# A decoder step with stick-breaking attention: keys moved to partitions, later keys summed by triangular products, and the order of products in every weight multiplication

## What is computed

```
z          = q . k / sqrt(64)
log_keep   = log_sigmoid(-z)                      # = -(max(z,0) + ln(1 + exp(-|z|)))
after[s]   = sum of log_keep over the keys between s and t
weight[s]  = exp(log_sigmoid(z) + after)          # = exp(z + log_keep[s] + after[s])
out        = sum over s of weight[s] * v[s]
```

## Time and profile before

| | us |
|---|---|
| median of 3 runs | 2714.1 (2711.0 to 2717.55) |
| the profiled execution, its own time | 2701.8 |
| its span, first to last instruction | 2700.0 |
| attention of layer 1 and head norm (from the last matmul of the gemm before to the first of the output gemm) | 1888.8 to 2146.6 |
| of that, stick-breaking units | about 1964 to 2128 |
| mean granted TensorE clock, share of full | 0.962 |

### The profile page before, as it was taken

One profiled execution on the slowest core, in us unless ns is written; L12 is line 12 of the kernel. 1 busy time (PEld: TensorE's weight loads), 2 busy tenths in 40 slices (PEclk: granted clock), 3 DMA queues, 4 the chain that ended last, 5 costly groups with the idle time before them and its releaser, 6 DMA issues. The chain is left out here.

```text
span 2700.0 us, 44621 instructions
## 1 busy us (share of the span) xinstructions
PE 2566.6 (95%) x18322; PEld 2437.0 (90%) x18322; DVE 884.3 (33%) x1549; ACT 773.1 (29%) x963; POOL 807.9 (30%) x204
## 2 busy tenths in 40 slices
PE   7999999997789999999999999999788799999997
PEld 7999999985589999999999999999455599999997
DVE  3221223686742211223322022211655432202234
ACT  4222223223123222224322122311444432212232
POOL 3333333320023333433333333333000033333332
PEclk9999999997789999999999999999887799999998
DMA  4222223411112222222222222333321022222122
GB/s 150 90 77 91 78 69 115 76 63 37 44 65 87 78 82 90 78 68 79 103 78 78 102 78 69 108 118 125 107 85 48 15 88 78 69 98 82 61 87 74
DMA packets 66901, 220.57 MB, mean 82 GB/s; under 512 B 14006, under 2 KB 31286, under 8 KB 51194
## 3 DMA queue, kind: packets, MB, share of 16 engines
q1 hardware_dynamic: 55968, 202.35, 21.7%
q10 hardware_dynamic: 10842, 16.96, 2.2%
HBM read 207.95 MB, written 11.33 MB: 81 GB/s over the span
## 5 line engine op out<-in xcount | busy, mean ns | idle before, releaser
L439 POOL TENSOR_TENSOR wl<-raw,wr 128x2048 fp32r<-128x2048 f32 (+2 forms) x200 | 807.7, 4038 | 1866.8 <-ACT wr L868 1866.8
L449 PE MATMUL ps<-xr,wr 128*128 128x256 f32 (+1 forms) x2432 | 726.2, 299 | 27.5 <-POOL wl L439 20.2
L451 PE MATMUL ps<-xr,wl 128*128 128x256 f32 (+1 forms) x2432 | 723.3, 297 | 0.0
L450 PE MATMUL ps<-xl,wr 128*128 128x256 f32 (+1 forms) x2432 | 723.1, 297 | 0.0
L449 PEld LDWEIGHTS ps<-xr,wr 128*128 128x128 f32 x2432 | 464.5, 191 | 31.3 <-issue 24.2
L449 PE MATMUL ps<-x2r,wr 128*128 128x256 f32 (+1 forms) x1664 | 491.3, 295 | 0.8 <-POOL wl L439 0.8
L451 PE MATMUL ps<-x2r,wl 128*128 128x256 f32 (+1 forms) x1664 | 489.7, 294 | 0.0
L450 PE MATMUL ps<-x2l,wr 128*128 128x256 f32 (+1 forms) x1664 | 489.4, 294 | 0.0
L450 PEld LDWEIGHTS ps<-xl,wr 128*128 128x128 f32 x2432 | 464.4, 191 | 0.2
L451 PEld LDWEIGHTS ps<-xr,wl 128*128 128x128 f32 x2432 | 463.9, 191 | 0.0
L868 ACT ACTIVATE wr<-raw 128x2048 fp32r<-128x2048 f32 (+1 forms) x200 | 351.5, 1758 | 372.5 <-PE ps L451 299.1
(11 more groups left out here) (310 smaller groups left out, 1857.9 us busy)
## 6 DMA issues: line engine op xcount, KB each, us to landing
raw<-in_up SPq DMA_DIRECT2D x88, 1024.0 KB, 4.8
raw<-in_down SPq DMA_DIRECT2D x32, 768.0 KB, 4.1
raw<-in_mixin SPq DMA_DIRECT2D x24, 1024.0 KB, 4.8
raw<-in_down SPq DMA_DIRECT2D x32, 640.0 KB, 3.8
raw<-in_ple SPq DMA_DIRECT2D x16, 640.0 KB, 3.9
raw<-in_mixout SPq DMA_DIRECT2D x8, 1024.0 KB, 5.0
kc<-in_kc SPq DMA_DIRECT2D x32, 256.0 KB, 3.7
vc<-in_vc SPq DMA_DIRECT2D x32, 256.0 KB, 4.0
```

Source lines behind the costliest of these rows:

```text
L439: e.tensor_tensor(wl[s][:, 0:p.width], raw[s][:, 0:p.width], wr[s][:, 0:p.width].bitcast(F32), ALU.subtract).then_inc(S(f"w_split{s}"), 1)
L449: e.matmul(out, wrt, xrt, start=first, stop=False)
L450: e.matmul(out, wrt, xlt, start=False, stop=False)
L451: return e.matmul(out, wlt, xrt, start=False, stop=last)
```

## The change

Stick-breaking attention is recast with the 128 keys on partitions and queries in columns, both heads of a pair in one unit: 20 units in place of 36. For a block of keys `i` the queries from that block on are its columns (512 - 128 i). The running sum along keys becomes products on PE: a triangular matrix `after` within the block and a matrix of minus ones `later` for each later block, accumulated in PSUM; DVE adds the sums to the logits, ACT takes exp, and the weights are already in the layout for the product with the values, which now gives feature-major output. Transposes, their copies and the scan go away. The mask is added by DVE when it copies the scores out of PSUM. For the sample group the cached keys and values are the stationary operand (128 x 128) and 16 or 32 query columns stream. The head norm of the differential half is cut in six parts of 384 columns and worked inside the ticks of stick-breaking, and so are the rounding and rest of its four tiles; the output gemm reads `okr`, `oql`, which lie over `ok` and `oq`, in place of `xr`, `xl`.

In every gemm the six matmuls of a step are issued in another order: for wr·xr, then wr·xl, then wl·xr, the first bank and the second bank each. The constants are loaded in two parts; the second is loaded by SP ahead of the bias strips in layer 1. Cache jobs 6 and 7 wait for stick-breaking's own units.

```diff
-                            for hf in range(2):
-                                x0, x1 = (0, CUT) if hf == 0 else (CUT, T)
-                                mm = mm3(piece(u, hf), wr[s][:, a:b], wl[s][:, a:b],
-                                         r[:, x0:x1], q[:, x0:x1], k == 0, k == kn_ - 1)
+                            for n_, (w_, x_) in enumerate(((wr[s], r), (wr[s], q), (wl[s], r))):
+                                for hf, (x0, x1) in enumerate(((0, CUT), (CUT, T))):
+                                    mm = e.matmul(piece(u, hf), w_[:, a:b], x_[:, x0:x1],
+                                                  start=k == 0 and n_ == 0, stop=k == kn_ - 1 and n_ == 2)
...
+    UNITS = [(hh, i) for hh in range(HEADS) for i in (3, SAMPLES, 2, 1, 0)]
+    OC_AT, OC_COLS = (6, 7, 11, 12, 16, 17), 3 * P
...
-                e.wait_ge(S("values_done"), SAMPLE_AT[job - 2] + 1)
+                if job < PAIRS + 2:
+                    e.wait_ge(S("values_done"), SAMPLE_AT[job - 2] + 1)
+                else:
+                    e.wait_ge(S("stick_values"), STICK_AT[job - 2 - PAIRS] + 1)
...
+        def stick_scores(v):
...
+            if i < SAMPLES:
+                for c in range(2):
+                    r = slice(64 * c, 64 * c + 64)
+                    mm = e.matmul(ps[:, s + c, 0:w], ok[1][r, hh, i * P:(i + 1) * P], oq[1][r, hh, i * P:SEQ],
+                                  start=True, stop=True)
+            else:
...
+                for g in range(NPG):
+                    for h_ in range(HEADS):
+                        for b in range(2):
+                            o, q = g * P + h_ * 32 + b * 16, h_ * P + (2 * hh + b) * 16
+                            e.matmul(ps[:, s, o:o + 16], kc[job % 2][:, b, h_, g, :], qst[:, q:q + 16],
+                                     start=True, stop=True)
...
+        def stick_sums(v):
...
+            if i < SAMPLES:
+                for j in range(i, TM):
+                    o, at = (j - i) * P, STICK_COLS[j]
+                    for c in range(2):
+                        mm = e.matmul(ps[:, s + c, o:w], C("after" if j == i else "later"),
+                                      stick[hh % 2][:, c, at:at + w - o], start=j == i, stop=j == TM - 1)
+            else:
+                for g in range(NPG + 1):
+                    for q in range(g, NPG + 1):
+                        mm = e.matmul(ps[:, s, g * P:(g + 1) * P], C("after" if q == g else "later"),
+                                      stick_s[:, q * P:(q + 1) * P], start=q == g, stop=q == NPG)
...
+        def stick_values(v):
...
+                for o0, o1 in ((0, P), (P, w))[:TM - i]:
+                    for c in range(2):
+                        f = (2 * hh + c) * 64
+                        mm = e.matmul(ps[64 * c:64 * c + 64, 6, i * P + o0:i * P + o1], ov[1][:, i, f:f + 64],
+                                      wt[:, c, o0:o1], start=i == TM - 1, stop=i == 0 and o0 > 0)
```

The order of the calls in a tick, with k = tick - 20, on PE:

```diff
+        for tick in range(TICKS.stop):
...
+                stick_scores(k)
...
+                stick_sums(k - 2)
...
+                stick_values(k - 3)
+            if k in OC_AT:
...
+                e.matmul(oc_ps, ones[:], sq[:, 0:OC_COLS], start=True, stop=True).then_inc(S("oc_ss"), 1)
```

On ACT, where `stick_soft(k, 0)` is |z|, `stick_soft(k, 1)` is exp and ln, and `stick_weights(k - 2)`, the exp, waits for `stick_add(k - 2)` of DVE:

```diff
+        for tick in range(TICKS.stop):
...
+                stick_soft(k, 0)
...
+                stick_weights(k - 2)
...
+                stick_soft(k, 1)
...
+        for j in range(HEADS, KD):
+            mix_round(j)
```

On DVE, where `stick_logs` makes -log_keep once the ln is there and `stick_add` adds the sums of PE to the logits:

```diff
+        for tick in range(TICKS.stop):
...
+                stick_mask(k)
...
+                stick_out(k - 4)
...
+                stick_logs(k - 1)
...
+                stick_add(k - 2)
```

More of the change, by code:

```diff
@@ L51, with offsets @@
 BLK = 2048
[L54 to L62, removed]
+CONST = dict(ident=128, cm=128, blk_ml=64, blk_col=8, sel=4 * 128)
+CONST2 = dict(neg_incl=128, dneg=4 * 64, fold=64, half0=1, half1=1, stick_neg=128, own_neg=4 * 32,
+              after=128, later=128)
+def offsets(widths):
+    at, o = {}, 0
+    for n, w in widths.items():
+        at[n] = o
+        o += w
+    return at, o
+COFF, CW = offsets(CONST)
+COFF2, CW2 = offsets(CONST2)
 PARAM = dict(gains=9 * KD, conv_w=TM * TAPS, conv_b=TM, ln_g=TM, ln_b=TM, gate_b=2, head_g=TM,
@@ L219, in build @@
     ov = [sb(f"ov{i}", [P, ST, DA], at=z) for i in range(2)]
+    STRIP_AT = z[0]
     strip = sb("strip", [P, HEADS, SEQ], at=z)
@@ new lines, in build, with width1, of_unit, logits @@
+    N1 = len(UNITS)
+    STICK_AT = [v for v, m in enumerate(UNITS) if m[1] == SAMPLES]
+    TICKS = range(N, N + N1 + 5)
+    OC_AT, OC_COLS = (6, 7, 11, 12, 16, 17), 3 * P
+    def width1(v):
+        i = UNITS[v][1]
+        return 3 * P if i == SAMPLES else SEQ - i * P
+    def of_unit(v, banks):
+        w = width1(v)
+        return banks[:, 0, 0:w] if UNITS[v][1] == SAMPLES else banks[:, :, 0:w]
+    def logits(v):
+        return of_unit(v, stk[v % 4][:])
+    def keep_logs(v):
+        hh, i = UNITS[v]
+        return stick_s[:] if i == SAMPLES else stick[hh % 2][:, :, STICK_COLS[i]:STICK_COLS[i] + width1(v)]
@@ L734, in turn_rows @@
+        def turn_rows(u):
+            src, w, bank = rows[u % 4], width(u), 4 + u % 2
+            e.wait_ge(S("probs_done"), u + 1)
+            if u >= 2:
+                e.wait_ge(S("probsT_copied"), u - 1)
+            for b in range((w + P - 1) // P):
                 wb = min(P, w - b * P)
-                if other is None:
-                    mm = e.transpose(ps[0:wb, 4 + u % 2, b * P:(b + 1) * P], src[:, b * P:b * P + wb], C("ident"))
+                if MAPS[u][1] < SAMPLES:
+                    mm = e.transpose(ps[0:wb, bank, b * P:(b + 1) * P], src[:, b * P:b * P + wb], C("ident"))
@@ L844, in _ @@
+        e.wait_ge(S("stick_weights"), N1)
+        e.wait_ge(S("oc_root"), 2 * len(OC_AT))
+        gemm(("out", 1), lambda tile, k: (okr[k // TM][:, k % TM, :], oql[k // TM][:, k % TM, :]), lambda tile, k: ("mix_ready", KD + k + 1) if tile == 0 else None)
         ffn(3, 6)
@@ new lines, in stick_add, with stick_logs @@
+        def stick_add(v):
+            e.wait_ge(S("stick_sums"), v + 1)
+            e.tensor_tensor(logits(v), logits(v), of_unit(v, ps[:, 4:6, :]), ALU.add).then_inc(S("stick_added"), 1)
+        def stick_logs(v):
+            hh, i = UNITS[v]
+            e.wait_ge(S("stick_soft"), 3 * v + 3)
+            if i == TM - 1 and hh >= 2:
+                e.wait_ge(S("stick_sums"), UNITS.index((hh - 2, 0)) + 1)
+            if i == SAMPLES and hh:
+                e.wait_ge(S("stick_sums"), STICK_AT[hh - 1] + 1)
+            e.scalar_tensor_tensor(keep_logs(v), logits(v), 0.0, of_unit(v, soft1[v % 2][:]), ALU.max, ALU.add
+                                   ).then_inc(S("stick_logs"), 1)
@@ L1833, in _ @@
+        for j in range(HEADS, KD):
+            mix_rest(j)
         out_and_norm(("out", 1), 6)
```

575 lines of the change are left out of this document (324 added, 251 removed).

## The result

| | us |
|---|---|
| before, median of 4 runs | 2714.9 (2711.0 to 2717.6) |
| after, median of 4 runs | 2670.8 (2667.4 to 2675.0) |
| ratio | 0.9839, 95% interval 0.9821 to 0.9858 |
| profiled execution, before | 2701.8 |
| profiled execution, after | 2675.0 |

The change is 44 us faster by the medians, 26.8 by the two profiled executions; the forecast was 25 by either. Of the 17 us between the two counts, 13 lie with before, whose profiled execution is that far under its median, and 4 with after, whose profiled execution is its slowest.

What follows compares the result with a forecast made beforehand. PE bounds the gemms; in stick-breaking no engine is full and units go round a ring of engines. First pair to 2000, three periods of 36, end 2123.5 against 2146.6, plus 1.9 of clock: 25 saved, 2689 us, range 2650 to 2718.

Steps and rivals of the forecast that it cites:

- The end's term: After the last period: sums at partly half clock 10, add, exp, values 4.5, changes 1; 2108 to 2123.5.
- The first pair's total: First stick-breaking pair with the rest of differential attention: 28 us from 1972.4, to about 2000.
- rival 1: The clock holds in stick-breaking: period 27.6, first pair 22, end 12, total 2655; chance 0.16.
- the warm start of the output gemm: Output gemm's first 3.8 us were at half clock; PE coming in warm gives 1.9 us back.
- the rate that the prediction took: Half-clock cost per period: 2 x 10.3 us would cost 10.3, taken as 8.4 since DVE and ACT partly set the pace.
- Its stretches behind the blocks: A half-clock stretch of 10.3 us behind each of a period's two blocks of 16-column products.
- which lengthen the ring below by some 0.7 us per head: Head norm's six parts inside the ticks: PE 3.9 us in all, ACT an ln and exp per part.
- the ring: Chain of DVE and ACT passes setting the pace within a period: 7.2 us, with handoffs 7.7, PE's work hidden.
- I take the saving over to the median: The 25 us saving, summed on the profiled execution, is subtracted from the median: 2714.1 - 25 = 2689.
- rival 3: Gemm matmul order costs 1 ns or more each, +17 us, 2706, or gains as much, 2672; chance 0.10.
- 2, half clock never lifts: In stick-breaking, sample blocks keep half clock: period 47, first pair 36, end 19, total 2735; chance 0.10.
- 4, dropped loads: In the gemms four of six equal-weight loads are dropped: 13 ns x 11,136 = 145 us, 2545; chance 0.02.

Runs made afterwards that it cites:

- f_after: The changed kernel run once more, unchanged: 2672.6 us, ratio 0.9865.
- e8: The changed kernel with sample scores and values streaming 128 columns in place of 16 and the own-values product over 128 rows: 2658.8 us, ratio 0.9804.
- e6: The changed kernel with the head norm's six parts behind the last unit in place of inside the ticks: 2675.9 us, ratio 0.9878.
- e9: e8 with the norm's parts at the places of e3: 2650.3 us, ratio 0.9783.
- e4: The changed kernel with sample scores over cached keys streaming 128 columns in place of 16: 2673.0 us, ratio 0.9874.
- e10: e8 with the sample scores at 16 columns again, values still wide: 2667.3 us, ratio 0.9841.
- e5: e4 with the sample values streaming 128 columns too, ordered by column: 2669.0 us, ratio 0.9860.
- e1: The kernel before with only the gemm's new order of the six matmuls: 2706.3 us, ratio 0.9985.
- e3: The changed kernel with the norm's parts in ticks 5, 7, 10, 12, 15, 17 in place of 6, 7, 11, 12, 16, 17: 2670.6 us, ratio 0.9853.

## Why the prediction was right, and where its terms were off

**Place and sum.** First pair done at 1998.6 (forecast 2000), periods of 36.8 and 36.9 (36), output gemm at 2124.4 (2123.5), warm as forecast. The end's term stands: 14.2 us behind the last sample values, forecast 15.5. The first pair's total stands by luck: its first product comes at 1975.2 in place of 1972.4, and from there it takes 23.4 us in place of 28, since its two blocks, costed at 8.5 and 6.5, take 4.2 and 4.7 at full clock. That is near the 22 of rival 1. Of the 26.8 us saved by profile 21.7 lie in the gap; of the other 5.1 the warm start of the output gemm is 1.9, the rest was not traced.

**The period: two errors that cancel.** The two periods of f_after hold the same work of PE at different clocks. A mean of 0.78 is half clock for 2 x 0.22 of the time, so 38.48 us hold 16.9 us of it, and 34.33 at 0.90 hold 6.9. That is 4.15 us for 10.0 us of half clock, 0.41 each, the rate that the prediction took (8.4 for 20.6). Taken back to full clock by it, the change's period is 31.5, an estimate from these rows; e8, with some 0.7 us more of values, shows 31.9. The prediction had 27.6. Its stretches behind the blocks were 20.6 us a period; the period at 2040.84 shows 13.6, some 5.5 us of cost in place of 8.4, and of these only 10.2 stand behind a block, the values', and 3.4 behind the norm's wait. So +3.9 and -2.9 came to 36.9 against 36. That these cancel is luck.

**The step that was mis-sized is the norm's**, "which lengthen the ring below by some 0.7 us per head". Without the norm e6's period of 31.31 at 0.84 comes to 27.2 at full clock by the same rate, beside the 26.9 that the prediction has without its 0.7. With it, 31.5: two parts a period cost about 4 us at full clock, and the half clock behind the wait by the same rate some 1.4 more. It was costed by PE's columns and ACT's passes. An estimate from the rows comes near the 4: two products of 384 columns at the prediction's 1.68 ns are 1.3 us, and PE's wait for the one buffer, which was put at nothing, is 2.55. In e8, at full clock, the ring from the start of the wide add (DVE, 2020.56) to the end of the sample unit's add (2031.46) is 10.9 us where the prediction had 7.7, and that wait stands in it. In e9, where PE waits 1.3, it is 9.3 and the period 1.0 shorter than in e8's first.

**The clock.** That blocks of 16 columns would be followed by half clock although PE has no gap, read from L656, held: e4 takes it away behind the scores by nothing but more columns, e10 behind the values, e5 and e8 behind both (e5, e8 and e10 also regroup the values). Its size did not: a longer stretch of 10.3 us behind each block was forecast, and the eight blocks of after show 0 to 10.2 us, 5.5 in the mean. The Trainium skill (TensorE: Matmul & The Clock Gate, Loop structure matters more than you think) has matmuls that come back to back stay warm, and go cold in long DMA waits. By that the change would have run warm in its blocks. The trace disagrees for the blocks of 16 columns, with 6.8 us at 0.50 behind the gapless one at 2030.12, and agrees for e9, whose blocks stream 128: 1.00 in both periods. That half clock follows a wait fits the 3.4 us behind the norm's, though this one is a wait of 2.55 us for ACT.

**Saving carried to the median.** By profile 26.8 against 25. The step that made 2689 out of it, "I take the saving over to the median", is where some 17 of the 18 us to 2670.8 were lost: the profiled execution of before lies 13.1 us under its median, that of after 4.2 above. What sets the median of before that far above its profile was not tried, so this part of the 44 us has no shown cause.

**Rivals.** The median alone would not have told them apart: 2670.8 is 18 us from the forecast, 16 from rival 1's 2655 and at rival 3's 2672. The traces do. 1, the clock holds: no, 0.81; and e9 and e8 show that with full clock the period is 31 to 32, not 27.6, so its 2655 had the norm's error whole. 2, half clock never lifts: no. 3, the order: a gain of 17 us is outside e1's interval; up to 10 is inside. 4, dropped loads: no, 18,370 of each; its 13 ns a matmul no run shows. PE did not wait for cached keys: the sample scores at 2040.84 have no idle time before them.

## What to carry to other kernels

Work that is moved off the end of a chain into a loop is not free because the engines there have idle time: look at which buffer it shares and who stands behind its wait, and try it at the end as well. Its wait can cost clock too: after shows 3.4 us at half clock behind each of three waits of 2.55 us, e3 and e9 none behind six of 1.3. A block of products whose time is set by weight loads can stream more columns for nothing, and should, where the rows show half clock behind it; but keep the array's shape the same through the block. And before a saving is carried from a profile to the median, see where the profiled execution lies among the runs, by its time and its granted clock.

## What the runs showed of the hardware

- An fp32 matmul instruction with a 128 x 128 load took 0.117 us at full clock with 16 columns (3.75 / 32) and 0.118 with 128 (3.77 / 32). The Trainium skill (TensorE: Matmul & The Clock Gate, LDWEIGHTS (loading the stationary operand)) gives a load of P weight columns as P / 1.2 ns, an estimate of 107 for 128; the time per instruction in the rows is a tenth above it.
- Alternating products over 64 and over 128 rows of the array cost 0.39 us per pair of changes: a group of e5 takes 1.06 us, one of e8 0.67 for the same six instructions. That is the prediction's 0.2 us a change. e8's values at full clock, with the group's own (920) and the cached ones (923) in one shape:

```profile
2034.54 0.61 PE L923 MATMUL ps<-stk,vc 128*128 128x128 f32 x4
2034.98 0.39 PE L920 MATMUL ps<-stk,ov 128*128 128x128 f32 x2
2035.21 0.61 PE L923 MATMUL ps<-stk,vc 128*128 128x128 f32 x4
```
